# A two-block transformer kernel on one core: low parts ahead of scores in its last mixer, and softmax maps divided on GpSimd in its first

## The reference, cut to what matters

```
# first block: mixer
qa, ka, va, qk_b, vb, ob, ib, fb, ga, gb = split(rms_norm(h) @ w_in)
ya = attention(rope(qa), rope(ka), va)            # 8 heads of 64, causal: softmax(q k^T) v
hb = mlstm(silu(conv(qk_b)), vb, ib, fb)          # 4 heads of 128, one chunk
merged = sigmoid(ga) * (ya @ w_proj_a) + sigmoid(gb) * (yb @ w_proj_b)
h = h + merged @ w_out ;  h = h + ffn(h)
# second block, layer 1: mixer
s = q k^T ; p = softmax(s) for both halves of a head
a = p[0] - lam * p[1] ;  o = a @ v                # 6 heads of 128
o_m = softmax(q_m k_m^T) v_m                      # 4 heads against 256 memory rows
x = x + concat(o, o_m) @ w_out
```

## Time and profile before

| | us |
|---|---|
| median of 3 runs | 1374.20 |
| lowest and highest | 1373.98, 1375.94 |
| the profiled execution, its whole time | 1373.87 |
| its span, first to last instruction | 1372.1 |
| TensorE busy | 1360.8 |
| VectorE busy | 942.9 |
| ScalarE busy | 713.5 |
| GpSimd busy | 126.8 |

### The profile page before, as it was taken

How to read it: one execution, slowest core, us unless ns; L and a number is a source line. 1 busy time by engine, 2 the same in 40 slices (tenths; PEclk the granted TensorE clock), 3 DMA queues, 4 the chain that set the end, 5 groups by cost and what they waited for, 6 DMA issues and landing times.

```text
span 1372.1 us, 19177 instructions
## 1 busy us (share of the span) xinstructions
PE 1360.8 (99%) x7393; PEld 1160.7 (85%) x7393; DVE 942.9 (69%) x1174; ACT 713.5 (52%) x943; POOL 126.8 (9%) x147
## 2 busy tenths in 40 slices
PE   9999999999999999999999999999999999999999
PEld 7988888888888888887788888888888877888887
DVE  6894667666677666768666666766667778676665
ACT  5556436444464444577664444544445677544442
POOL 4000002000030000042020000200000332200000
PEclk9999999999999999999999999999999999999999
DMA  8644457655546655553346556566555442565662
GB/s 272 196 158 147 154 184 264 227 183 189 199 158 205 198 184 183 176 185 131 124 153 214 184 184 194 163 203 197 192 184 184 161 147 94 165 202 184 187 198 74
DMA packets 164859, 246.34 MB, mean 180 GB/s; under 512 B 4952, under 2 KB 121860, under 8 KB 164672
## 3 DMA queue, kind: packets, MB, share of 16 engines
q1 hardware_dynamic: 162736, 240.19, 53.8%
q0 software_dynamic: 1776, 4.74, 1.2%
q10 hardware_dynamic: 288, 0.61, 0.1%
HBM read 244.45 MB, written 1.07 MB: 179 GB/s over the span
## 4 chain that ended last, share of the span: by engine, by line
PE 96%; DVE 2%; ACT 1%; issue 0%; DMA 0%; POOL 0%; ACTq 0%; DVEq 0%; POOLq 0%
PE ps L1624 29%; PE ps L1591 15%; PE ps L1629 15%; PE ps L1593 15%; PE ps L1592 15%; PE ps L1829 1%; PE ps L1881 1%; PE ps L1617 1%; DVE wlo L1473 1%; PE ps L2133 1%; PE ps L1865 0%; DMA gcol<-in_gcol 0%; ACT whi L608 0%; PE ps L1912 0%; PE ps L1918 0%
## 5 line engine op out<-in xcount | busy, mean ns | idle before, releaser
L1624 PE MATMUL ps<-xx,whi 128*128 128x512 f32 x1760 | 422.1, 391 | 0.0
L1624 PEld LDWEIGHTS ps<-xx,whi 128*128 128x128 f32 x1760 | 325.5, 188 | 64.4
L969 DVE TENSOR_TENSOR wlo<-raw,whi 128x2048 fp32r<-128x2048 f32 x120 | 275.1, 2293 | 94.4 <-ACT whi L616 94.4
L616 ACT ACTIVATE whi<-raw 128x2048 fp32r<-128x2048 f32 x120 | 229.6, 1913 | 122.7 <-PE ps L1593 122.4
L608 ACT ACTIVATE whi<-raw 128x2048 fp32r<-128x2048 f32 (+1 forms) x135 | 205.2, 1531 | 82.0 <-PE ps L1593 70.7
L1629 PEld LDWEIGHTS ps<-xx,wlo 128*128 128x128 f32 x1760 | 227.6, 191 | 9.9
L1629 PE MATMUL ps<-xx,wlo 128*128 128x256 f32 x1760 | 230.6, 283 | 0.0
L1591 PE MATMUL ps<-whi,hhi 128*128 128x512 f32 x504 | 198.8, 394 | 0.0
L1592 PE MATMUL ps<-wlo,hhi 128*128 128x512 f32 x504 | 196.8, 390 | 0.0
L1593 PE MATMUL ps<-whi,hlo 128*128 128x512 f32 x504 | 196.3, 390 | 0.0
L964 DVE TENSOR_TENSOR wlo<-raw,whi 128x2048 fp32r<-128x2048 f32 x75 | 171.5, 2288 | 31.0 <-ACT whi L608 30.9
(11 more groups left out here) (279 smaller groups left out, 1371.0 us busy)
## 6 DMA issues: line engine op xcount, KB each, us to landing
raw<-in_ffn_w_gate SPq DMA_DIRECT2D x44, 1024.0 KB, 5.3
raw<-in_ffn_w_up SPq DMA_DIRECT2D x44, 1024.0 KB, 5.3
raw<-in_ffn_w_down SPq DMA_DIRECT2D x44, 1024.0 KB, 5.0
raw<-in_w_in SPq DMA_DIRECT2D x40, 1024.0 KB, 5.1
raw<-in_w_gate_up SPq DMA_DIRECT2D x22, 1024.0 KB, 5.1
raw<-in_w_out SPq DMA_DIRECT2D x12, 1024.0 KB, 5.0
raw<-in_w_down SPq DMA_DIRECT2D x11, 1024.0 KB, 5.0
raw<-in_w_mem_kv SPq DMA_DIRECT2D x4, 1024.0 KB, 5.1
```

Source lines behind the costliest of these rows:

```text
L616: act.activation(whi[:, c % 3, :], raw[:, c % 3, :], ACT.Copy).then_inc(hi_done, 1)
L969: dve.tensor_tensor(wlo[:, c % 3, :], raw[:, c % 3, :], whi[:, c % 3, :], ALU.subtract)\
L1624: return pe.matmul(ps[:, bank + n, :], whi[:, slot, 256 * k + P * n:256 * k + P * n + P], both, start=start, stop=False)
```

## The change

1. **Last mixer (layer 1).** In slots 25 and 29 VectorE makes the first half of the unit's low part ahead of the scores, the second half one slot later (`LO_SOON`), so that slots 27 and 31 have none. `rotated(6)` goes from slot 30 to 31 (`ROTATED`). Combine of items 2 and 3 goes from slot 32 to 31, that of items 14 and 15 from 52 to 51 (`C_AT`). The product of items 8 and 9 goes from slot 46 to 47 (`V_AT`). On ScalarE the squares of the sub-norm come first in their slot, and in slot 51 the exponentials come behind `evac_pT` (`E_LATE`).
2. **First mixer.** The A items come in the order of head pairs, both row blocks after each other. GpSimd takes the inverse of the row sums by a power of -1 and divides each map by two tensor_scalar instructions (one a head). An A item is turned two units behind its scores and its product follows three units behind; items 8 and 9 catch up, item 8 turned in the middle of unit 17. The product has v as the stationary side (64 wide) and `pT` as the moving one (128 columns), so that it comes out turned (as L1865 does it in layer 0). It goes from bank 7 to `hhi` and `hlo` at k = 6 and 10. The reciprocals, the multiplication into `xn` and eight transposes of it go.
3. One more constant (`mone`) is set on GpSimd at the start, ahead of its first DMA.

```
-ITEMS = [("A", rt, a, -1) for rt in range(RT) for a in range(AH // 2)]
+ITEMS = [("A", rt, a, -1) for a in range(AH // 2) for rt in range(RT)]
-DIRECT = [layer == 0 for *_, layer in ITEMS]
+DIRECT = [k == "A" or layer == 0 for k, _, _, layer in ITEMS]
-C_AT = (28, 32, None, None, 44, 47, 50, 52)
+C_AT = (28, 31, None, None, 44, 47, 50, 51)
+E_LATE = 51
+LO_SOON = (25, 29)
 V_AT = (...
-        (30, 30, 34, 34, 38, 38, 42, 42, 46, 46, 49, 49, 52, 52, 54, 54))
+        (30, 30, 34, 34, 38, 38, 42, 42, 47, 47, 49, 49, 52, 52, 54, 54))
+ROTATED = {14: 2, 16: 3, 31: 6, 32: 7, 38: 8, 40: 9}
...
# GpSimd
+            pool.memset(mone[:, :], -1.0).then_inc(pool_chain, 1)
             pool.memset(mhalf[:, :], -0.5).then_inc(pool_chain, 1)
...
+            for i in range(8):
+                nk = P * (ITEMS[i][1] + 1)
+                total = sums[:, 2 * i:2 * i + 2]
+                pool.wait_ge(p_ready, SOFT[i])
+                pool.tensor_tensor(total, total, mone[:, :].to_broadcast([P, 2]), ALU.pow).then_inc(inv_ready, 1)
+                pool.wait_ge(inv_ready, i + 1)
+                for e in range(2):
+                    v = maps(i)[:, SEQ * e:SEQ * e + nk]
+                    ins = pool.tensor_scalar(v, v, total[:, e:e + 1], None, ALU.mult)
+                ins.then_inc(pn_ready, 1)
...
# ScalarE, first mixer
+                if u == 17:
+                    evac_pT(8)
...
-                    if 1 <= k <= 12:
+                    if 2 <= k <= 9:
+                        evac_pT(k - 2)
+                    if 10 <= k <= 12:
                         evac_pT(k - 1)
                     if k < 8:
                         exps(k)
+                    if k in (6, 10):
+                        b = (k - 6) // 4
+                        act.wait_ge(pv_ready, 4 * b + 4)
+                        act.activation(hhi[:, b, :], ps[:, 7, :], ACT.Copy).then_inc(xhi_done, 2)
...
# VectorE, first mixer
-                    if k in (5, 9):
-                        link(dve.reciprocal(rec[:, 0:8], sums[:, 2 * i:2 * i + 8]))
-                        dve.wait_ge(pv_ready, i + 4)
-                        dve.tensor_tensor(xn[:, r, 0:512]..., ps[:, 7, :]..., rec[:, 0:8]..., ALU.mult)
+                    if k in (6, 10):
+                        b = (k - 6) // 4
+                        dve.wait_ge(xhi_done, KC * T_Y0 + 2 * b + 2)
+                        dve.tensor_tensor(hlo[:, b, :], ps[:, 7, :], hhi[:, b, :], ALU.subtract).then_inc(xlo_done, 2)
...
# VectorE, last mixer
+                    if L == 1 and h in LO_SOON:
+                        lo_half(u + (h + 7) // 4, 0)
                     for i in items_at(S_AT[L], h):
                         scores(i0 + i)
...
# TensorE, first mixer
                     if k < 12:
                         item_scores(k)
-                    if 1 <= k <= 12:
+                    if 3 <= k <= 10:
+                        item_pv(k - 3)
+                    if k == 11:
+                        item_pv(8)
+                    if 11 <= k <= 13:
+                        item_pv(k - 2)
+                    if 2 <= k <= 9:
+                        item_turn(k - 2)
+                    if 10 <= k <= 12:
                         item_turn(k - 1)
-                    if 2 <= k <= 13:
-                        item_pv(k - 2)
-                if u == 19:
-                    pe.wait_ge(sc_read, 12)
-                    pe.wait_ge(o_evac, 2)
-                    turn_part(T_Y0, 0, xn)
-                    turn_part(T_Y0, 1, xn)
```

More of the change, by code:

```diff
@@ L934, in _ @@
                         ins.then_inc(sub_sq, 1)
+                    if h != E_LATE:
+                        for i in items_at(E_AT[L], h):
+                            exps(i0 + i)
+                    if h in (4, 8):
+                        act.wait_ge(unit_used, u + h // 4)
+                        turned_gain(T, n, h // 8)
+                    if (h + 8) % 4 < 2:
+                        c = u + (h + 8) // 4
+                        hi(c, c % 3, h % 4)
+                    for i in items_at(T_AT[L], h):
+                        evac_pT(i0 + i)
+                    if h == E_LATE:
+                        for i in items_at(E_AT[L], h):
+                            exps(i0 + i)
+                    if h < 48 and h % 8 in (5, 7):
+                        tile_out(2 * (h // 8) + (h % 8 == 7))
                     if h in HEAD_TURNS:
@@ L1571, in _ @@
                         memory_out()
[L1572 to L1575 removed]
+                    if L == 1 and h in ROTATED:
+                        rotated(ROTATED[h])
+                    m, part = (h + 6) // 4, (h + 6) % 4
+                    if L == 1 and h - 1 in LO_SOON:
+                        lo_half(u + m, 1)
+                    elif L == 1 and h - 2 in LO_SOON:
+                        pass
+                    elif h >= 2 and part < 2:
+                        lo_half(u + m, part)
                 boundary(T_F2 + 3 * L, N_F2 + 3 * L, R_WO1 + 3 * L, WO[1 + L] + 3, None, FFU[2 + 2 * L])
@@ L1664, in row_scales, with narrow @@
                 ins.then_inc(rb_ps, 1)
-            def narrow(u, slot, bank, T=None):
+            def narrow(u, slot, bank, T=None, turned=None):
                 pe.wait_ge(lo_done, u + 1)
@@ L1674, in narrow, with wide @@
                                     k == 0, k == KC - 1)
+                    if n == 0 and turned is not None:
+                        item_turn(turned)
                 ins.then_inc(unit_used, 1)
-            def wide(u, half, banks, free):
+            def wide(u, half, banks, free, turned=None):
                 pe.wait_ge(lo_done, u + 1)
@@ L1685, in wide @@
                                     half == 0 and k == 0, half == 1 and k == 3)
+                    if r == 0 and turned is not None:
+                        item_turn(turned)
                 ins.then_inc(unit_used, 1)
@@ L1937, in free @@
                     return (cin_done if which == "cin" else stream_evac), value
+                turned = 8 if u == 17 else None
                 if QKB <= u < VB:
@@ L1940, in _ @@
                         pe.wait_ge(*free(tiles))
-                    narrow(u, u % 3, tiles % 4)
+                    narrow(u, u % 3, tiles % 4, turned=turned)
                     tiles += 1
@@ L1946, in _ @@
                     else:
-                        wide(u, u % 2, (tiles % 4, (tiles + 1) % 4), (free(tiles), free(tiles + 1)))
+                        wide(u, u % 2, (tiles % 4, (tiles + 1) % 4), (free(tiles), free(tiles + 1)),
+                             turned)
                     tiles += 2 * (u % 2)
@@ L2035, in _ @@
                 pe.wait_ge(lo_done, u + 1)
+                if m == 0:
+                    pe.wait_ge(sc_read, 12)
                 if m == 1:
```

59 lines of the change are left out of this document (17 added, 42 removed).

## The result

The changed kernel takes 1367.15 us in the median of 5 runs (1366.66 to 1368.14), the kernel before, run beside it, 1374.2 (1373.31 to 1375.94). The ratio is 0.9947, with a 95% interval of 0.9935 to 0.9959. 7.05 us are won, where 5.6 were forecast; the time lies in the range given. How much of the 7.05 is the forecast's mechanism, and how much something it left out, the experiments tell. The profiled execution took 1366.66 us, 1364.9 of it in its span.

The account below looks back on a forecast made before the run. TensorE's work plus its few waits was taken as the bound. The last mixer's 3.9 us and the first mixer's 1.7 us made 5.6 us won, a median of 1368.6 us, range 1366.3 to 1372.0.

Parts of the forecast that it names:

- item 0 and item 2: Last mixer: TensorE's waits at these items' turns go, 0.82 us in full and 2.86 of 2.92 us.
- VectorE's backlog: Last mixer: two rotations delay the scores of items 4 and 5 by 2 us; costed at nothing, up to 1 us.
- Item 8: Last mixer: the product's 0.76 us wait goes, but item 10's turn then waits; 0.44 us won.
- Items 13 and 14: Last mixer: item 13's 0.58 us wait goes, item 14's turn comes later; a loss of 0.19 us.
- The wait at 75.64: First mixer: item 1's turn waits for exponentials of the same slot; this 0.4 us goes.
- Products of kind A: First mixer: four r = 1 products in turned form win 0.9 us; 0.6 taken, between 0.4 and 1.2.
- may lose 0.06 us a time: First mixer: possible loss from the turned product standing in front of the transposes.
- The cover of 10 us: First mixer: time left between scores and turn, two units apart, to hide GpSimd's 2.8 us an item.
- rival E: First mixer: GpSimd becomes the bound from 7.0 us an item; 14 us slower, 1382.6 us; chance 0.05.
- C: Last mixer: the reordering does nothing, waits move by a slot, only the first mixer wins; 1372.5 us; chance 0.08.
- D: First mixer: VectorE loses all of GpSimd's time, 7.5 us of waits for scores; 1376.1 us; chance 0.05.
- B: Last mixer: VectorE's backlog behind slot 31 brings back 1.5 to 3 us; 1370.1 to 1371.6 us; chance 0.15.

Follow-up runs that it names:

- no_soon: The changed kernel with its two low halves ahead of the scores of slots 25 and 29 put back behind them; 1369.23 us.
- exps_first: The changed kernel with the exponentials of items 14 and 15 ahead of the copy of item 13's turn again; 1366.32 us.
- turn_first: The changed kernel with the turn of a map ahead of the turned product in each slot of the first mixer; 1368.17 us.
- pool_6: The changed kernel with GpSimd multiplying each divided map of the first block five times more by 1.0; 1407.59 us.
- pool_2: The changed kernel with GpSimd multiplying each divided map of the first block once more by 1.0; 1367.64 us.
- control_before: The kernel before, unchanged, run again beside the two parts alone; 1375.56 us in one run.
- control_after: The changed kernel, unchanged, run again beside the two parts alone; 1367.00 us in one run.
- first_only: The changed kernel with its last mixer as before; 1372.19 us, ratio 0.9985 to the kernel before.
- last_only: The changed kernel with its first mixer as before; 1369.68 us, ratio 0.997 to the kernel before.

## Why the prediction was right, and where its sizes were off

*What bounds the kernel.* Right: VectorE's, ScalarE's and GpSimd's changes counted only at TensorE's waits. 24 us more on GpSimd cost nothing.

*Last mixer, item 0 and item 2.* 0.82 and 2.86 us were forecast; 0.82 and 2.87 went. The cover named for VectorE's backlog, the three slots between the scores of items 4 and 5 and their turns with 0.8 us left, held: TensorE has no wait there. `no_soon` shows how near it was. With one more low half in the backlog it fails, and what I costed "at up to 1 us if that cover fails" came to 1.2 us.

*Item 8.* 0.44 us forecast, 0.35 measured, the new wait before the turn of item 10 being 0.42 us. My working gives 0.30 by its own figures: the turn at 1152.66 less TensorE's arrival at 1152.2 is a wait of 0.46, and 0.76 - 0.46 = 0.30. *Items 13 and 14:* a loss of 0.19 forecast, 0.22 measured (1.64 us for 1.42). The cause I named, exponentials that wait for item 13's turn, is confirmed by `exps_first`, which gives back 1.0 us without them. The waits sum to 3.8 us, the stage shows 3.74, the forecast was 3.9.

*What was missing.* The clock. I took the profile's full clock as given for every execution. In two of three profiles the wait of item 2 also costs 1.5 us of half-speed work behind it, and 23 of the 34 executions of the kernel before that ran beside the experiments have a mean clock under 1.000. This, and not a larger saving of waits, is why the median fell by 4.76 us with the last mixer's part alone. It is also most of what the whole forecast missed: from the full-clock executions of the kernel before (1373.07) to the changed kernel (1367.15, not run beside them) it is 5.9 us, where 5.6 were forecast, and the rest of the 7.05 is the price of the clock. The range held it because it had room for larger savings of waits, which is luck as far as the clock goes.

*First mixer.* 1.7 us forecast, 2.25 measured. Transposes: 0.79 us, as read. The wait at 75.64: 0.34 of 0.4. Item 8 turned inside unit 17: it took 0.23 us there and 0.22 in its old slot, so the 0.15 I took off was not lost. Products of kind A: 4.72 us before, 3.84 after, 0.88 won where 0.9 less a loss was taken as 0.6. An item with r = 1 took 0.59 us, the estimate. The term that was mis-sized is the last one, "may lose 0.06 us a time": I set it for the turned form in front of the transposes, but the change also moves the turns behind the product. By kind, the turns took 4.24 us before and 3.47 after, a gain of 0.77, and the mLSTM items' scores and products 0.5 us more, since they now stand in front of other neighbours. `turn_first` isolates it: with the old order the mixer would have been 101.89 - 100.67 = 1.22 us shorter, less than my 1.7, and the order adds 1.03. The loss that I priced at 0.06 us a time is 0.10 there: two transposes took 0.37 us in front of a turned product and 0.27 in front of the old one, four took 0.58 and 0.49. So 1.7 came near 2.25 by two misses of opposite sign, a loss that was priced too low and a gain from the order that I had not priced at all. That is luck.

*What must hide.* GpSimd took 3.2 us an item, above the 2.0 and 2.8 forecast and under the 6.6 allowed; 256 columns cost 0.94 us each alone, inside the bounds. None of these pairs grew to 3 us an instruction, as I had said of those that meet a low part: the longest pair of 256 columns took 2.06 us, since it was mostly the power that met the low part (up to 2.26 us); one pair of 128 columns took 3.05. The cover of 10 us held for items 2 to 7 (power of item 2 at 77.40, its turn at 87.98), but not for the first two: GpSimd gets item 1 at 74.56 and TensorE turns it at 80.84, 6.3 us later. That was enough for its 2.8 us. VectorE lost 0.9 us, under the bound of 3.7. The point from which rival E decides, 7.0 us an item, stands: 6.95 by `pool_6`.

*The range.* Its lower end is mis-added: all five waits, 5.9 us, and 2.6 us of the first mixer lead from 1374.2 to 1365.7, not 1366.3. The result lies above both.

*The rivals.* C fell (the waits went). D fell with `pool_2`. E is real but lies beyond 6.95 us an item. B doesn't occur in the changed kernel, and does as soon as the pulled-up halves go.

*The start.* 1.1 us of the two profiles' difference lie before the first scores, in neither part of the change. The rows of DMA issues from 0 to 9 us show a load that ScalarE's first copies need; in the kernel before they wait for it for 4.1 us. Here it is in the kernel before and then in the changed one (KB, us from issue to landing):

```profile
gcol<-in_gcol POOLq DMA_DIRECT2D x1, 44.0 KB, 5.5
```

```profile
gcol<-in_gcol POOLq DMA_DIRECT2D x1, 44.0 KB, 4.2
```

It landed 1.3 us earlier. In other profiles it took 5.8 us (`control_before`), 4.6 (`control_after`), 5.4 (`first_only`, which has the constant `mone`) and 5.2 (`last_only`, `exps_first`). So the constant isn't the cause. Nor is this load the only one that counts: in `last_only` the first large product waited for a high part whose `raw` had come late. The first large product came at 7.5 to 8.4 us in ten profiles with both parts and at 8.6 to 8.9 in four without one of them; whether that is more than scatter stays open. The medians leave no room for it: 1373.07 less the two stages, 3.74 and 2.25, is 1367.08, and the changed kernel took 1367.15.

## What to carry to other kernels

A wait of TensorE has two prices: its own length, and what the clock takes behind it in part of the executions; look at the granted clock behind each long wait in more than one profile. When a step is pulled ahead on a busy engine, ask which idle time pays for it; here the earlier combine and the later rotation removed the long wait, and the pulled-up halves kept the backlog from coming back. The order of small products between two dense units is worth as much as their number: put those whose change-over is cheap next to the dense unit, and price a moved instruction in front of its new neighbour.

## What the runs showed of the hardware

- Behind 2.72 and 2.76 us of idle time TensorE's granted clock fell to 0.50 (1.2 GHz), for some 3 us, and behind another 2.76 us it stayed at full; behind 1.48 us (nine profiles) and 1.66 us (one) it did not fall. It fell behind all five waits in the profile of `pool_6`, 2.6 to 8.1 us long. One fall cost 1.5 us.
- GpSimd waits for VectorE and hardly the other way: a low part of 2048 columns takes 2.29 us with or without GpSimd's work, whichever started first, while two tensor_scalars of GpSimd beside it take 3.96 us instead of 1.89.
- A power of 128x2 on GpSimd takes 0.72 us alone and 2.26 where it meets a low part; a tensor_scalar of 256 columns 0.94 us.
- Four transposes of 128x128 cost 0.41 or 0.58 us from start to start, by what stands behind them (a dense matmul, or the turned product), and 0.49 in front of a product in the old form.
